# Two softmax attentions with the scores one turn earlier, and transposes and copies signalled one head at a time

## The chip, the core and the metric

The kernel runs on one core of a Trainium2 chip. TensorE (PE), VectorE (DVE), ScalarE (ACT), GpSimd (POOL) and SyncE (SP) each work through a queue of their own, in order, and wait for one another through counting semaphores. The metric is the device time of one execution in microseconds (us). A profiled execution gives, beside that, the start and the duration of every instruction.

## What is computed

Two transformer blocks run one after the other on 512 tokens of width 1024. The first block has, among other things, a chunked attention with a relative bias (8 heads, here called the first attention); the second has a windowed attention with shared keys and a sink (16 heads, the second attention). Both are a softmax over scores plus a table, times values:

```python
# first block, per head; bias is looked up by clipped distance, valid masks chunks ahead
scores = jnp.einsum('bhcqd,bhckd->bhcqk', qc, kb)
scores = jnp.where(valid[None, None, :, None, :], scores + bias[None, :, None], -jnp.inf)
probs = jax.nn.softmax(scores, axis=-1)
out = jnp.einsum('bhcqk,bhckd->bhcqd', probs, vb)
...
# second block, per block of 128 queries
logits = jnp.einsum('bqkgd,bskd->bkgqs', qi, ks).astype(jnp.float32) * scale + bias
logits = jnp.where(valid, logits, NEG_INF)
m = jnp.maximum(logits.max(-1), sink_f)
p = jnp.exp(logits - m[..., None])
denom = p.sum(-1) + jnp.exp(sink_f - m)
o = jnp.einsum('bkgqs,bskd->bqkgd', p, vs.astype(jnp.float32))
o = o / denom.transpose(0, 3, 1, 2)[..., None]
```

Around them stand dense layers (projections, a gated feed-forward layer, a convolution branch) and a product-key expert layer, which together take most of the time and which the change does not touch.

## The kernel before

Weights come from memory as a stream of 128x1024 slots through a ring of four buffers; ACT and POOL split each slot into a high and a low part, and PE multiplies three times for each product. All stages run one after the other in one program. During the two attentions the stream stands still, since its ring is full and nothing consumes it: POOL has nothing to do there, and the engines at work are PE, DVE and ACT.

An attention is a list of *pairs*. A pair is two heads (called halves 0 and 1) and one block of 128 queries. Four pairs (query blocks 0 to 3) make a *group*. In the first attention there are 16 pairs, and the number of keys n of a group's pairs is 128, 256, 384 and 512. In the second there are 32 pairs with n of 256, 384, 384 and 256. All three engines run a loop over *turns*, and each turn works on several pairs at once, in an order written out by hand in three functions of the name `attention(st)`:

- **DVE**, turn p: for both halves *logit* (L862: adds the table to the scores in PSUM, writes `pr`, keeps the maximum), then the small steps on the maxima (L867, or L870 and L871 with a sink), which raise `maxed`; then for pair p-1 the reciprocal of the sum (L878) and *norm* (L881, two instructions, each raises `normed`). A logit waits for `score`, and, since `pr` has three buffers (`PAIRS_PR`), for `turned` of pair p-3.
- **ACT**, turn p: *exp* (L500, two instructions, plus L502 for a sink) of pair p once `maxed` is there; then *copy* (L512) of the transposed probabilities of pair p-2 from banks 6 and 7 (one bank for each half) to `pT`, after `turned` of that pair and `mixed` of pair p-4. The second copy raises `turned_sb`. After a group's last pair, ACT copies the finished heads out (L518). It also issues the DMA of the next group's table.
- **PE**, turn p: *scores* (L1353) of pair p into banks 4 and 5 or 0 and 1 by the parity of p, after the logits of pair p-2; *transposes* (L1364) of pair p-2 into banks 6 and 7, after `turned_sb` of pair p-3 (the banks are free) and `normed` of its own half; *mix* (L1375, probabilities times values) of pair p-3 after `turned_sb` of that pair.

Since each queue is in order, a wait of one instruction holds everything behind it. On PE that means: scores of pair p+1 come behind the transposes of pair p-2 and the mix of pair p-3.

Of the kernel before, what the change touches and what calls it, by code (L numbers as in the profile page):

```python
# [26 lines left out]
ACT = mybir.ActivationFunctionType  # L27
AX_X = mybir.AxisListType.X

P = 128  # L30
# [93 lines left out]
PAIRS_PR = 3  # L124
# [37 lines left out]
def program(nc, x, stream, gains, consts, rel, gqa, keys, ohc, out):  # L162
    ctx = ExitStack()
    with ctx:
# [282 lines left out]
        def _(act):  # L447
# [39 lines left out]
            def attention(st):  # L487
                s, pairs, sm = st["s"], st["pairs"], st["sm"]
                n = len(pairs)
                for p in range(n + 4):  # L490
# [13 lines left out]
                    v = p - 2  # L504
                    if 0 <= v < n:
                        w = pairs[v]
                        act.wait_ge(s["turned"], v + 1)
                        if v >= 2:

                            act.wait_ge(s["mixed"], v - 1)  # L510
                        for half in (0, 1):
                            e = act.activation(st["pT"][:, v % 2, half, :w["n"]], B[6 + half][:, :w["n"]], ACT.Copy)  # L512
                        e.then_inc(s["turned_sb"], 1)
                    v = p - 4
                    if v >= 0 and v % TT == TT - 1:
                        w = pairs[v]
# [273 lines left out]
        def _(dve):  # L790
# [54 lines left out]
            def attention(st):  # L845
                s, pairs, sm = st["s"], st["pairs"], st["sm"]
                n = len(pairs)
                for p in range(n + 1):
                    if p < n:
# [7 lines left out]
                        dve.wait_ge(s["score"], p + 1)  # L857
                        if p >= PAIRS_PR:

                            dve.wait_ge(s["turned"], p - PAIRS_PR + 1)  # L860
                        for half in (0, 1):
                            dve.tensor_tensor_reduce(out=st["pr"][:, p % PAIRS_PR, half, :w["n"]], in0=B[SCORES[p % 2][half]][:, :w["n"]],  # L862
                                                     in1=st["tbl"][g % 2][:, half, w["c0"]:w["c0"] + w["n"]], scale=1.0, scalar=-3.0e38,
# [380 lines left out]
        def _(pe):  # L1244
# [98 lines left out]
            def attention(st):  # L1343
                s, pairs = st["s"], st["pairs"]
                n = len(pairs)
                for p in range(n + 3):
                    if p < n:
                        w = pairs[p]
                        if p >= 2:

                            pe.wait_ge(s["logit"], 2 * p - 2)
                        for half in (0, 1):
                            m = pe.matmul(B[SCORES[p % 2][half]][:, :w["n"]], st["qk"][ROWS[half], w["q"], w["i"] * P:(w["i"] + 1) * P],  # L1353
                                          st["qk"][ROWS[half], w["k"], w["k0"]:w["k0"] + w["n"]], start=True, stop=True)
                        m.then_inc(s["score"], 1)
                    v = p - 2
                    if 0 <= v < n:
                        w = pairs[v]
                        if v >= 1:
                            pe.wait_ge(s["turned_sb"], v)  # L1360
                        for half in (0, 1):
                            pe.wait_ge(s["normed"], 2 * v + half + 1)
                            for c in range(0, w["n"], P):
                                m = pe.transpose(B[6 + half][:, c:c + P], st["pr"][:, v % PAIRS_PR, half, c:c + P], ident)  # L1364
                        m.then_inc(s["turned"], 1)
                    v = p - 3
                    if v >= 0:
                        w = pairs[v]
                        pe.wait_ge(s["turned_sb"], v + 1)
                        if w["group"] >= 2 and v % TT == 0:  # L1370
                            pe.wait_ge(s["head_out"], w["group"] - 1)
                        nb = w["n"] // P
                        for b in range(nb):
                            for half in (0, 1):
                                m = pe.matmul(B[2 + w["group"] % 2][ROWS[half], w["i"] * P:(w["i"] + 1) * P],  # L1375
                                              st["v"][:, w["k0"] // P + b, w["v"][half]:w["v"][half] + HD],
                                              st["pT"][:, v % 2, half, b * P:(b + 1) * P], start=b == 0, stop=b == nb - 1,
                                              skip_group_check=True)
                        m.then_inc(s["mixed"], 1)
# [375 lines left out]
```

## Time and profile before

| | us |
|---|---|
| time, median of 3 runs (lowest to highest) | 2940.41 (2938.57 to 2943.82) |
| the profiled execution's own time | 2938.94 |
| its span from first to last instruction | 2937.1 |
| PE busy over the span | 2767.3 (94%) |
| DVE busy | 1657.0 (56%) |
| ACT busy | 841.9 (29%) |
| POOL busy | 1157.6 (39%) |
| first attention, from its first logit to its last copy-out | 268.7 to 319.3 |
| second attention, likewise | 1085.5 to 1179.4 |

Busy shares over the whole span say little about the attentions, which are 5% of it. A line of the timeline reads: start and duration in us, engine, source line, operation, output tile <- input tiles, shape, how many instructions were merged, and in brackets the idle time of the engine before it and what ended that. Matmuls overlap in the pipeline, so that the time from the start of one group of matmuls to the start of the next (its pitch) says more than their durations. PEld is PE's weight load, which runs beside the matmuls.

### The profile page before, as it was taken

Reading aid. Unit: us, or ns where it says so; the run is one execution under the profiler, and the core shown is the slowest. Engines: PE = TensorE matmul, PEld = TensorE weight load, DVE = VectorE, ACT = ScalarE, POOL = GpSimd, SP = SyncE. Lnnn points to the kernel's source line nnn. Section 1 sums busy time; section 2 is a strip of 40 time slices with the busy share of each in tenths; the row PEclk is TensorE's granted clock in tenths of the full one; section 3 lists DMA queues with packets and bytes.
Section 4 is the critical chain, followed back from the end, with each engine's and each line's share of the span. In section 5 each row is a group of like instructions: output and inputs, shape, how many; then the busy total and the mean of one; then the engine's idle time right before and its main releaser. Section 6 shows DMA issues by size and latency. Waiting matters only on the chain.

```text
span 2937.1 us, 38574 instructions
## 1 busy us (share of the span) xinstructions
PE 2767.3 (94%) x13164; PEld 2188.6 (75%) x13164; DVE 1657.0 (56%) x3297; ACT 841.9 (29%) x1285; POOL 1157.6 (39%) x976
## 2 busy tenths in 40 slices
PE   6997899999999987999999999999999999999997
PEld 5863478878788764778777777888888888888775
DVE  4135642111599537469999956444444444444787
ACT  1133323322222427123445521222222222222111
POOL 4410155555455430453410044444444444444442
PEclk9988999999999999999999999999999999999998
DMA  4210033323223220222346764443443443443442
GB/s 141 88 36 22 15 94 95 98 93 100 87 93 94 78 88 28 65 89 79 94 151 236 253 196 140 114 129 113 115 129 110 119 128 109 120 124 112 128 129 64
DMA packets 208200, 315.44 MB, mean 107 GB/s; under 512 B 139888, under 2 KB 142320, under 8 KB 203888
## 3 DMA queue, kind: packets, MB, share of 16 engines
q1 hardware_dynamic: 63792, 233.34, 25.5%
q10 hardware_dynamic: 144320, 80.94, 10.0%
q8 instruction: 53, 0.87, 0.1%
q14 instruction: 35, 0.29, 0.0%
HBM read 275.45 MB, written 38.80 MB: 107 GB/s over the span
## 4 chain that ended last, share of the span: by engine, by line
PE 43%; issue 23%; DVE 18%; POOL 14%; ACT 1%; DMA 0%; DVEq 0%; ACTq 0%; POOLq 0%
POOL lo L431 14%; PE bank L1247 14%; PE bank L1248 14%; PE bank L1249 14%; DVE ohg L1173 3%; DVE bank L1200 1%; DVE oh L1169 1%; DVE oh L1170 1%; DVE WH L1202 1%; DVE lo L1181 1%; DVE eq L1146 1%; DVE idx L1088 1%; DVE idx L1080 1%; DVE scb L1081 1%; PE bank L1364 1%
## 5 line engine op out<-in xcount | busy, mean ns | idle before, releaser
L431 POOL TENSOR_TENSOR lo<-raw,hi 128x256 fp32r<-128x256 f32 (+1 forms) x972 | 1157.4, 1218 | 1741.5 <-ACT hi L457 911.9
L1247 PE MATMUL bank<-inH,hi 128*128 128x512 f32 x2240 | 893.9, 399 | 28.4 <-DVE inL L798 15.9
L1248 PE MATMUL bank<-inL,hi 128*128 128x512 f32 x2240 | 879.9, 393 | 0.0
L1249 PE MATMUL bank<-inH,lo 128*128 128x512 f32 x2240 | 879.6, 393 | 0.0
L1208 DVE TENSOR_TENSOR xT<-xT,bank 128x512 f32<-128x512 f32 x504 | 339.6, 685 | 538.4 <-PE bank L1249 538.4
L1247 PEld LDWEIGHTS bank<-inH,hi 128*128 128x128 f32 x2240 | 425.6, 190 | 125.9 <-issue 32.9
L1249 PEld LDWEIGHTS bank<-inH,lo 128*128 128x128 f32 x2240 | 425.0, 190 | 90.7
L1248 PEld LDWEIGHTS bank<-inL,hi 128*128 128x128 f32 x2240 | 426.2, 190 | 88.1 <-issue 2.2
L1247 PE MATMUL bank<-WH,hi 128*128 128x512 f32 x1024 | 408.5, 399 | 14.9 <-DVE xT L1208 14.9
L1248 PE MATMUL bank<-WL,hi 128*128 128x512 f32 x1024 | 404.0, 395 | 0.0
L1249 PE MATMUL bank<-WH,lo 128*128 128x512 f32 x1024 | 400.5, 391 | 0.0
L457 ACT ACTIVATE hi<-raw 128x1024 fp32r<-128x1024 f32 x232 | 243.6, 1056 | 483.4 <-PE bank L1249 441.1
L726 ACT ACTIVATE hi<-raw 128x1024 fp32r<-128x1024 f32 x180 | 184.9, 1054 | 455.3 <-PE bank L1249 455.3
L1247 PEld LDWEIGHTS bank<-WH,hi 128*128 128x128 f32 x1024 | 192.2, 188 | 69.1 <-DVE xT L1208 23.6
L1249 PEld LDWEIGHTS bank<-WH,lo 128*128 128x128 f32 x1024 | 192.0, 188 | 48.3
L1248 PEld LDWEIGHTS bank<-WL,hi 128*128 128x128 f32 x1024 | 192.2, 188 | 42.1
L1200 DVE TENSOR_TENSOR bank<-A,Gd 128x512 f32<-128x512 f32 x128 | 142.5, 1114 | 18.1 <-DMA Gd<-gates 15.0
L1008 DVE SCALAR_TENSOR_TENSOR bank<-u,gn,bank 128x512 f32<-128x512 f32 x224 | 148.2, 748 | 0.0
L737 ACT ACTIVATE A<-bank 128x512 f32 (+1 forms) x84 | 50.3, 599 | 318.5 <-PE bank L1249 196.7
L978 DVE TENSOR_TENSOR rt<-sq,bank 128x512 f32<-128x512 f32 x22 | 15.1, 688 | 177.0 <-PE bank L1249 177.0
L961 DVE TENSOR_TENSOR xT<-xT,bank 128x512 f32<-128x512 f32 x24 | 16.5, 687 | 138.5 <-PE bank L1249 138.3
L1202 DVE TENSOR_SCALAR WH<-bank 128x512 fp32r<-128x512 f32 x128 | 88.5, 692 | 4.4
(205 smaller groups left out, 2430.3 us busy)
## 6 DMA issues: line engine op xcount, KB each, us to landing
raw<-stream SPq DMA_DIRECT2D x440, 512.0 KB, 3.6
Gd<-gates ACTq DMA_DIRECT2D x32, 1024.0 KB, 7.4
gates<-stage_a ACTq DMA_DIRECT2D x16, 1024.0 KB, 4.3
gates<-stage_b ACTq DMA_DIRECT2D x16, 1024.0 KB, 4.2
tbl<-gqa ACTq DMA_DIRECT2D x8, 384.0 KB, 3.3
spilled<-res ACTq DMA_DIRECT2D x12, 256.0 KB, 3.1
A<-spilled ACTq DMA_DIRECT2D x6, 512.0 KB, 3.7
xT<-x SPq DMA_DIRECT2D x1, 2048.0 KB, 8.8
```

What stands on the lines that cost most here:

```text
L431: ins = pool.tensor_tensor(lo[:, r, part], raw[:, r, part], hi[:, r, part].bitcast(F32), ALU.subtract)
L457: act.activation(hi[:, r % RING, :], raw[:, r % RING, :], ACT.Copy).then_inc(hi_done, 1)
L726: act.activation(hi[:, r, :], raw[:, r, :], ACT.Copy).then_inc(hi_done, 1)
L737: act.activation(A[:, bass.ds(slot + e, 1), :].rearrange("p a t -> p (a t)"), B[6 + e][:, :], ACT.Gelu).then_inc(gelu_done, 1)
L1008: done.append(chain.mark(dve.scalar_tensor_tensor(to, *tap(j), d, ALU.mult, ALU.add)))
L1173: ins = dve.tensor_tensor(ohg[:, r, part, :, :, :], oh1[:, :, :, :], by_key(gpart[:, part, tok]), ALU.mult)
L1200: chain(dve.tensor_tensor(w[:, :].rearrange("p (b t) -> p b t", t=SPILL), a, Gd[:, buf, :, 2 * wpar + e, :], ALU.mult))
L1202: chain(dve.tensor_scalar(h, w[:, :], 1.0, None, ALU.mult))
L1208: dve.tensor_tensor(xT[:, k, :], xT[:, k, :], B[k % 4][:, :], ALU.add).then_inc(y_added, 1)
L1247: pe.matmul(bank, wh, xh, start=start, stop=False)
L1248: pe.matmul(bank, wh, xl, start=False, stop=False)
L1249: return pe.matmul(bank, wl, xh, start=False, stop=stop_)
```

## The change

PE's loop starts one turn earlier (at -1) and issues the scores of pair p+1 in turn p, ahead of the transposes of pair p-2, still after the logits of the pair that used the same banks (p-1). The scores are then three turns ahead of the transposes instead of two.

Transposes raise `turned` once for each half instead of once for a pair, and ACT's copy of a half waits for its own half alone, and raises `turned_sb` for it. PE's transposes of a half wait for the copy of that half of the pair before. Waits for a whole pair count twice as far. DVE's program keeps its order; one of its waits has another number. No arithmetic changes, and no instruction that computes is added or taken away.

```diff
@@ ACT, attention @@
                         w = pairs[v]
-                        act.wait_ge(s["turned"], v + 1)
                         if v >= 2:
 
                             act.wait_ge(s["mixed"], v - 1)
                         for half in (0, 1):
-                            e = act.activation(st["pT"][:, v % 2, half, :w["n"]], B[6 + half][:, :w["n"]], ACT.Copy)
-                        e.then_inc(s["turned_sb"], 1)
+                            act.wait_ge(s["turned"], 2 * v + half + 1)
+                            act.activation(st["pT"][:, v % 2, half, :w["n"]], B[6 + half][:, :w["n"]], ACT.Copy).then_inc(s["turned_sb"], 1)
@@ DVE, attention @@
                         if p >= PAIRS_PR:
 
-                            dve.wait_ge(s["turned"], p - PAIRS_PR + 1)
+                            dve.wait_ge(s["turned"], 2 * (p - PAIRS_PR + 1))
@@ PE, attention @@
-                for p in range(n + 3):
-                    if p < n:
-                        w = pairs[p]
-                        if p >= 2:
-
-                            pe.wait_ge(s["logit"], 2 * p - 2)
+                for p in range(-1, n + 3):
+                    if p + 1 < n:
+                        w, b = pairs[p + 1], (p + 1) % 2
+                        if p >= 1:
+
+                            pe.wait_ge(s["logit"], 2 * p)
                         for half in (0, 1):
-                            m = pe.matmul(B[SCORES[p % 2][half]][:, :w["n"]], st["qk"][ROWS[half], w["q"], w["i"] * P:(w["i"] + 1) * P],
+                            m = pe.matmul(B[SCORES[b][half]][:, :w["n"]], st["qk"][ROWS[half], w["q"], w["i"] * P:(w["i"] + 1) * P],
                                           st["qk"][ROWS[half], w["k"], w["k0"]:w["k0"] + w["n"]], start=True, stop=True)
                         m.then_inc(s["score"], 1)
                     v = p - 2
                     if 0 <= v < n:
                         w = pairs[v]
-                        if v >= 1:
-                            pe.wait_ge(s["turned_sb"], v)
                         for half in (0, 1):
+                            if v >= 1:
+                                pe.wait_ge(s["turned_sb"], 2 * v + half - 1)
                             pe.wait_ge(s["normed"], 2 * v + half + 1)
                             for c in range(0, w["n"], P):
                                 m = pe.transpose(B[6 + half][:, c:c + P], st["pr"][:, v % PAIRS_PR, half, c:c + P], ident)
-                        m.then_inc(s["turned"], 1)
+                            m.then_inc(s["turned"], 1)
                     v = p - 3
                     if v >= 0:
                         w = pairs[v]
-                        pe.wait_ge(s["turned_sb"], v + 1)
+                        pe.wait_ge(s["turned_sb"], 2 * v + 2)
```

What stands in PE's queue in the second attention, in the turn that transposes a pair of 256 keys (n of 256, its two halves in banks 6 and 7). Before, with the mix and the next scores behind it:

```order
L1353 MATMUL bank4<-qk2_77 128x384 [waits logit2]
L1353 MATMUL bank5<-qk2_77 128x384
L1364 MATMUL bank6<-cs_56,pr2_81 128x128 [waits normed2,turned_sb2]
L1364 MATMUL bank6<-cs_56,pr2_81 128x128
L1364 MATMUL bank7<-cs_56,pr2_81 128x128 [waits normed2]
L1364 MATMUL bank7<-cs_56,pr2_81 128x128
L1375 MATMUL bank2<-pT2_82,v2_78 64x128 [waits turned_sb2]
L1375 MATMUL bank2<-pT2_82,v2_78 64x128 x3
L1353 MATMUL bank0<-qk2_77 128x256 [waits logit2]
L1353 MATMUL bank1<-qk2_77 128x256
```

Now (the same lines of code stand one number lower):

```order
L1352 MATMUL bank0<-qk2_77 128x256 [waits logit2]
L1352 MATMUL bank1<-qk2_77 128x256
L1363 MATMUL bank6<-cs_56,pr2_81 128x128 [waits normed2,turned_sb2]
L1363 MATMUL bank6<-cs_56,pr2_81 128x128
L1363 MATMUL bank7<-cs_56,pr2_81 128x128 [waits normed2,turned_sb2]
L1363 MATMUL bank7<-cs_56,pr2_81 128x128
L1374 MATMUL bank2<-pT2_82,v2_78 64x128 [waits turned_sb2]
L1374 MATMUL bank2<-pT2_82,v2_78 64x128 x3
L1352 MATMUL bank4<-qk2_77 128x256 [waits logit2]
L1352 MATMUL bank5<-qk2_77 128x256
```

The scores into banks 0 and 1, which stood behind these transposes and this mix, now stand ahead of them, and the second half's transposes have a second wait.

ACT's queue in the second attention, from a pair's last exp (L502) over the two copies to the next pair's exp. Before:

```order
L502 ACTIVATE sm2_85<-sm2_85 128x2
L512 ACTIVATE pT2_82<-bank6 128x256 [waits mixed2,turned2]
L512 ACTIVATE pT2_82<-bank7 128x256
L500 ACTIVATE pr2_81,sm2_85<-pr2_81,sm2_85 128x384 [waits maxed2]
L500 ACTIVATE pr2_81,sm2_85<-pr2_81,sm2_85 128x384
```

Now:

```order
L502 ACTIVATE sm2_85<-sm2_85 128x2
L512 ACTIVATE pT2_82<-bank6 128x256 [waits turned2,mixed2]
L512 ACTIVATE pT2_82<-bank7 128x256 [waits turned2]
L500 ACTIVATE pr2_81,sm2_85<-pr2_81,sm2_85 128x384 [waits maxed2]
L500 ACTIVATE pr2_81,sm2_85<-pr2_81,sm2_85 128x384
```

The order is the same; the second copy has a wait of its own.

## Rows read from the trace of the kernel before

**Rows 1.** Sums of each attention: stretch, length, each engine's busy us, clock, DMA.

```profile
268.70:319.30 50.60, 38.58 (x300) 23.38 (x296) 29.60 (x131) 31.70 (x100) 0.00 (x0) 0.91 0.07 22
1085.50:1179.40 93.90, 71.73 (x604) 44.23 (x600) 68.45 (x321) 66.37 (x233) 0.00 (x0) 0.96 0.09 27
```

**Rows 2.** Waits in the second attention: who waited for whom, total, times, longest.

```profile
PEld bank L1364 <- ACT pT L512: 34.3, 30, 2.6
...
DVE pr L862 <- PE bank L1353: 14.9, 21, 2.7
```

**Rows 3.** The chain of waits, second attention, in order of time: start, us, what.

```profile
1120.57 0.87 PE bank L1353 x4
...
1121.46 0.56 DVE pr L862
...
1124.33 0.55 ACT pT L512 x2
...
1124.92 0.66 PE bank L1364 x4
```

**Rows 4.** Timeline of DVE, second attention: first logit instruction of seven of its pairs.

```profile
1085.50 0.42 DVE L862 CUSTOM_DVE_ANT_0 pr<-bank,tbl 128x256 f32<-128x256 f32 x1 [0.86 <-PE bank L1353]
...
1086.58 0.55 DVE L862 CUSTOM_DVE_ANT_0 pr<-bank,tbl 128x384 f32<-128x384 f32 x1
...
1088.85 0.55 DVE L862 CUSTOM_DVE_ANT_0 pr<-bank,tbl 128x384 f32<-128x384 f32 x1
...
1091.25 0.42 DVE L862 CUSTOM_DVE_ANT_0 pr<-bank,tbl 128x256 f32<-128x256 f32 x1
...
1152.43 0.42 DVE L862 CUSTOM_DVE_ANT_0 pr<-bank,tbl 128x256 f32<-128x256 f32 x1 [1.06 <-PE bank L1353]
...
1163.67 0.42 DVE L862 CUSTOM_DVE_ANT_0 pr<-bank,tbl 128x256 f32<-128x256 f32 x1 [1.07 <-PE bank L1353]
...
1171.63 0.42 DVE L862 CUSTOM_DVE_ANT_0 pr<-bank,tbl 128x256 f32<-128x256 f32 x1
```

**Rows 5.** Timeline of PE, first attention, two stretches in which it hardly waited.

```profile
276.53 0.88 PE L1364 MATMUL bank<-cs,pr 128*128 128x128 f32 x6 [1.11 <-ACT pT L512]
277.33 0.66 PE L1375 MATMUL bank<-pT,v 128*64 128x128 f32 x8
277.92 0.70 PE L1353 MATMUL bank<-qk 64*128 64x256 f32 x4
278.55 1.09 PE L1364 MATMUL bank<-cs,pr 128*128 128x128 f32 x8
...
306.37 0.92 PE L1353 MATMUL bank<-qk 64*128 64x384 f32 x4
307.22 0.44 PE L1364 MATMUL bank<-cs,pr 128*128 128x128 f32 x2
```

**Rows 6.** Timeline of PE: first and last line of two stretches at the slower pace.

```profile
288.02 1.31 PE L1364 MATMUL bank<-cs,pr 128*128 128x128 f32 x6 [2.27 <-ACT pT L512]
...
292.59 0.88 PE L1375 MATMUL bank<-pT,v 128*64 128x128 f32 x12
...
1092.30 1.54 PE L1364 MATMUL bank<-cs,pr 128*128 128x128 f32 x6 [2.24 <-ACT pT L512]
...
1097.39 0.88 PE L1375 MATMUL bank<-pT,v 128*64 128x128 f32 x12
```

**Rows 7.** Timeline of DVE, first attention: first logit of pairs 0, 4 and 15.

```profile
268.73 0.29 DVE L862 CUSTOM_DVE_ANT_0 pr<-bank,tbl1a 128x128 f32<-128x128 f32 x1 [0.70 <-PE bank L1353]
...
275.56 0.29 DVE L862 CUSTOM_DVE_ANT_0 pr<-bank,tbl1b 128x128 f32<-128x128 f32 x1 [0.19 <-DVE tbl1b L856]
...
309.79 0.69 DVE L862 CUSTOM_DVE_ANT_0 pr<-bank,tbl1b 128x512 f32<-128x512 f32 x1 [0.48 <-PE bank L1353]
```

**Rows 8.** Timeline of ACT: the last pair's copies, first and second attention.

```profile
316.41 1.08 ACT L512 ACTIVATE pT<-bank 128x512 f32<-128x512 f32 x2 [1.18 <-PE bank L1364]
...
1177.35 0.66 ACT L512 ACTIVATE pT<-bank 128x256 f32<-128x256 f32 x2 [0.75 <-PE bank L1364]
```

## The prediction

> **What bounds the kernel now.** I read the sums of the two attentions first, then the waits in them, then the chain of waits, then the timelines of DVE and PE. The attentions take 50.6 and 93.9 us, and no engine is full there: in the second PE is busy for 71.7, DVE for 68.5 and ACT for 66.4 us of 93.9 [rows 1]. So a loop of waits sets the pace. The waits say which: PE's transposes stand for 34.3 us until ACT's copies free banks 6 and 7, and DVE's logits stand for 14.9 us until scores are there [rows 2]. The chain of waits closes the loop: scores start at 1120.57, the logits at 1121.46, the copies behind that pair's exps are under way at 1124.33, and the transposes start at 1124.92 [rows 3]. Behind the transposes stand a mix and the next scores, and only those let DVE go on. One such round is 1124.92 - 1120.57 = 4.35 us, plus transposes and mix of four and eight pieces, 2 x 0.59 (below) and a little issue time: about 5.6 us, and it moves the loop by two turns. That fits the 11.24 us which DVE needs for a group of four turns, from 1152.43 to 1163.67 [rows 4], or 2.81 a turn.
>
> **The change part by part.**
>
> *Scores one turn earlier.* The scores of pair p+1 no longer stand behind the transposes of p-2 and the mix of p-3. The path from DVE's logits over exp, copy, transposes, mix and scores back to DVE is as long as before but now moves the loop by three turns: 5.6 / 3 = 1.9 us a turn. It stops being the bound. What is late next is one of three queues, or the wait for a free `pr` buffer.
>
> DVE's queue, where it did not wait for scores: 2.27 us from 1086.58 to 1088.85 (logit 384, norm 256) and 2.40 to 1091.25 (384, 384) [rows 4]. A logit instruction of 256 is 0.13 shorter than one of 384 (0.42 against 0.55 [rows 4]), and there are two, so 256 with 384 is 2.40 - 0.26 = 2.14 and 256 with 256 is 2.27 - 0.26 = 2.01. A group: 8.82 us.
>
> PE's queue, by pitches where it did not wait: six transposes 0.80, a mix of eight 0.59, scores of 256 0.63, scores of 384 0.85 (306.37 to 307.22) [rows 5]. A mix of twelve and six transposes are both busy for 0.88 [rows 5, 6], a mix of eight and four transposes both for 0.66 [rows 3, 5], so I give them the same pitches. A pair of 256 costs 0.63 + 0.59 + 0.59 = 1.81, one of 384 0.85 + 0.80 + 0.80 = 2.45, a group 8.52 us. The first attention has the same mean n (320), so 8.52 there too. ACT: 66.4 / 8 = 8.3 and 31.7 / 4 = 7.9 us a group [rows 1], with small overlaps counted twice.
>
> The three queues are within 6% of each other, so that none will run quite without waits: the widths change from turn to turn, and an engine that is early in a narrow turn is late in a wide one. For that I add 0.2 us a group in the second attention, where DVE leads, and 0.6 in the first, where PE leads: 9.0 and 9.1 us a group.
>
> *The wait placed ahead.* Scores of p+1 wait for the logits of p-1, and the transposes of p-2, the mix of p-3 and through them ACT's copies are now queued behind that wait. It should be free: those transposes need norm of p-2, which on DVE comes after the logits of p-1. The scores' own 0.63 to 0.85 us delay the transposes by less than DVE takes between these logits and the end of that norm (max steps, reciprocal and norm, the rest of a turn of 2.4 us beyond about 1.1 us of logits).
>
> *Signals by half.* The added waits and increments are one each on PE and ACT a turn. In the trace PE already has a wait between the halves (for `normed`), and six transposes with it take 0.80 us, no more than a mix of twelve without, so a wait that is already met costs near nothing; the upper bound is the gap of 0.15 to 0.2 us that PE shows between a group of matmuls with a wait ahead and the one before (six transposes at 0.11 and a gap are 0.80). I take nothing, and keep 0.15 a turn for the range. For the increments the Trainium skill has a rule that speaks against this part (TensorE: Matmul & The Clock Gate, The cost: per-tile semaphore tail): increments serialize, at about 26 ns each. By it the 48 more would be worth 1.3 us at most; no row here shows an increment by itself. What the halves gain: the copy of half 0 starts while half 1 is still transposed, and the next transposes start after the first copy. In the loop this is slack. In the tail it is on the path: the last copies wait 1.18 and 0.75 us for transposes [rows 8], and the two last pairs run transposes and copies strictly in turn. I take 0.9 us from the first tail and 0.7 from the second.
>
> *The slow stretches.* At 288.02 PE needs 4.57 us until 292.59 for what otherwise takes 0.80 + 0.59 + 0.63 + about 1.0 = 3.0, and at 1092.30 5.09 until 1097.39 for 0.80 + 0.59 + 0.63 + 0.80 = 2.8 [rows 5, 6]. Both fit the lower of the two clocks (1.2 against 2.4 GHz), as do mean granted clocks of 0.91 and 0.96 [rows 1]. They cost 1.5 and 2.3 us of PE work; I take two stretches in the first attention (the mean clock has room for them), 3.0, and 2.3 in the second. Today part of that is slack; with PE nearly full it is all on the path. I assume that they stay.
>
> *Sum.* Second attention, first to last logit: now 1171.63 - 1085.50 = 86.1 us, of which 5.8 until 1091.25 is a start that doesn't wait [rows 4]. After: 5.8 + 7 x 9.0 + 2.3 = 71.1, so 15.0 less; with the tail 15.7 less. First attention: now 309.79 - 268.73 = 41.1, of which 6.8 until 275.56 [rows 7]. After: 6.8 + 2 x 9.1 + three turns of the last group (3/4 x 9.1 = 6.8) + 3.0 = 34.8, so 6.3 less; with the tail 7.2. Together 22.9 us. Nothing else fills that time: POOL and the weight stream stand still in both, so nothing they do later depends on how long the attentions take. The profiled execution goes from 2938.9 to 2916.0; the median of the runs is 1.5 above that execution, which gives 2917.5 us.
>
> **The rivals.**
>
> *PE becomes the bound.* If each added wait costs 0.15 us, PE's group is 8.52 + 4 x 0.15 = 9.1, and with 0.5 of unevenness 9.6 instead of 9.0 and 9.1: 7 x 0.6 + 2.75 x 0.5 = 5.6 us more, 2923. For it: PE is only 0.3 below DVE in a group. Against it: the pitch of six transposes with a wait between halves.
>
> *The buffer of `pr` becomes the bound.* Logit p waits for the transposes of p-3, that is logit p, exp p, copies of p-2, transposes of p-1, logit p+2. From 1121.46 to 1124.92 is 3.46 us, plus transposes of 0.66 [rows 3]: 4.1 for two turns, 8.2 a group, below DVE's 8.8. With widest pairs in a row it comes to some 4.5, against 4.67 of DVE for its two widest turns. If it binds at each group's wide turns, with 0.8 a group: 0.6 x 9.75 = 6 us more, again 2923; the two are told apart by who waits.
>
> *The lead does nothing.* Where PE's scores of p+1 still come late, since the mix of p-4 ahead of them waits for copies that come after the exp of p-2, only the halves help: some 0.3 us of copy and transposes in each round of two turns, 24 rounds, and the tails: 2940.4 - 7.2 - 1.6 = 2932. Against it: that mix belongs to a turn which is over when DVE reaches logit p-1, by the chain.
>
> *The clock (slower).* With PE at its lower clock a turn costs 2 x 8.52 / 4 = 4.26 us instead of 2.25, since PE is then the bound by far. Eleven or twelve turns more than now at that clock (23 / 2.0) eat the whole gain, and all 48 would end at some 3010. At 20 turns more the time is 2917.5 + 40 = 2958. What speaks for it is that slow stretches do come in the attentions, after PE has waited over 2 us [rows 6]; against it, that the change takes such waits away, and that between the stretches transposes run at their faster pitch. The Trainium skill (TensorE: Matmul & The Clock Gate, Part 4: PE-mode transpose) says that transposes don't count as work that holds the clock up. By that the denser loop would not hold the clock better, as about a third of its PE time is transposes; the trace has both attentions mostly at the higher clock with that same third.
>
> **How the numbers follow.** Forecast 0.70: 2917.5. PE bound or `pr` bound, 0.2 together: 2923. The lead does nothing, 0.04. Slower by the clock, 0.03. The rest, 0.03, is a gain beyond the range. The range: without any unevenness (0.2 x 7 + 0.6 x 2.75 = 3.1 us) and without slow stretches (5.3) the time is 2909; with the second or third case and one more slow stretch of 2.3 us elsewhere it is 2926. All but 0.1 lies between 2909 and 2926. A measurement of this kernel can tell about 0.2% (5.9 us) from no change, so faster means below 2934.5: 0.95. Same 0.02, slower 0.03.
>
> **What would show it.** In the new profile the logits' wait for scores (14.9 us in the second attention) should be nearly gone, and the transposes' wait for copies should fall from 34.3 to below 12. DVE's group in the second attention should be 8.8 to 9.2 us, with its longest idle in front of a logit below 0.4. PE's busy time in the attentions should stay the same in us. The second attention should last some 78 us, the first 43. I am wrong if PE shows idle in front of scores (its wait for logits), if ACT's copies wait for PE in mid-loop, if more of the attentions runs at the slower pitch, or if the groups fall to 9 us and the whole does not, which would mean that the slower clock came elsewhere.

## The result and the profile after

| | before | changed |
|---|---|---|
| median of the runs, us | 2939.5 (2938.6 to 2943.8, 4 runs) | 2907.9 (2906.1 to 2909.6, 4 runs) |
| the profiled execution's span | 2937.1 | 2907.7 |
| first attention, first logit to last copy-out | 50.6 | 39.9 |
| second attention, likewise | 93.9 | 74.4 |

The changed kernel takes 0.9884 of the time before, 95% interval 0.9869 to 0.9899: 31.6 us less where 22.9 were forecast. The direction and the mechanism were right; the time lies 1.1 us below the forecast range.

In the two profiles the attentions are 10.7 and 19.5 us shorter, 30.2 together, and the spans differ by 29.4. The other 0.8 us is a sum of both signs outside the attentions: 2.0 less ahead of the first logit, 1.1 more between the attentions, 1.6 more behind the second. That is code which the change does not touch. Yet the 1.1 us come again from profile to profile: over all thirteen profiles of this document, the part between the attentions takes 766.2 to 766.3 us in the three whose first attention runs as before, and 767.1 to 767.9 in the eight others with three `pr` buffers. In the 30.7 us behind the first attention the mean granted clock is 0.89 before and 0.83 in the changed kernel, so it is likely that a little of what the clock gives inside the attention is taken back behind it. The 1.6 us tell nothing: a second profile of the changed kernel has 3.5 us less there than the first.

The sums of the attentions (stretch, length, busy us of PE, PEld, DVE, ACT and POOL, granted clock, DMA share, GB/s), to be held against [rows 1]:

```profile
266.70:306.63 39.93, 35.11 (x300) 21.65 (x298) 29.63 (x131) 31.20 (x100) 0.00 (x0) 0.96 0.09 27
1073.96:1148.35 74.39, 68.08 (x604) 42.73 (x600) 66.16 (x320) 65.47 (x233) 0.00 (x0) 1.00 0.11 34
```

The instructions are the same and DVE and ACT are as long busy as before; what has gone is waiting. PE is busy for 3.5 us less in the first attention and 3.7 in the second, although it does the same work: the mean granted clock rose from 0.91 to 0.96 in the first attention and from 0.96 to 1.00 in the second, so that in the latter nothing is left of the stretch at the lower of the two levels (1.2 GHz). What keeps the first at 0.96 is a stretch that began ahead of it: the clock is 0.51 from 266.7 to 269.7 us and 1.00 from there to the attention's end.

The waits in the second attention, as in [rows 2]:

```profile
PEld bank L1363 <- ACT pT L512: 17.4, 31, 1.8
...
PE bank L1363 <- ACT pT L512: 4.0, 9, 1.4
...
DVE pr L861 <- PE bank L1352: 0.9, 1, 0.9
```

DVE's wait for scores fell from 14.9 us to one wait of 0.9, at the very start. PE's weight loads still wait 17.4 us for copies, and PE's matmuls 4.0: PE is now early and stands because DVE sets the pace. DVE's timeline shows that it does, first logits of two groups in a row, as [rows 4]:

```profile
1099.45 0.42 DVE L861 CUSTOM_DVE_ANT_0 pr<-bank,tbl 128x256 f32<-128x256 f32 x1
...
1101.45 0.55 DVE L861 CUSTOM_DVE_ANT_0 pr<-bank,tbl 128x384 f32<-128x384 f32 x1
...
1103.72 0.55 DVE L861 CUSTOM_DVE_ANT_0 pr<-bank,tbl 128x384 f32<-128x384 f32 x1
...
1106.12 0.42 DVE L861 CUSTOM_DVE_ANT_0 pr<-bank,tbl 128x256 f32<-128x256 f32 x1
...
1108.25 0.42 DVE L861 CUSTOM_DVE_ANT_0 pr<-bank,tbl 128x256 f32<-128x256 f32 x1
```

The turns are 2.00, 2.27, 2.40 and 2.13 us, a group 8.80, against 11.24 before, and no line has an idle time in brackets. All whole groups but the first (7.89) are like this to 0.01 us. The chain of waits agrees: between 1100 and 1110 us it lies on DVE from line to line, with ACT and PE nowhere in it (start, us, what):

```profile
1099.88 0.34 DVE pr L861
...
1100.92 0.36 DVE pr L880 x2
1101.28 0.17 issue
1101.45 0.55 DVE pr L861
```

In the first attention a group is 9.10 us, and there DVE still waits, in each group at the same places:

```profile
277.78 0.56 DVE L861 CUSTOM_DVE_ANT_0 pr<-bank,tbl1b 128x384 f32<-128x384 f32 x1 [0.89 <-PE bank L1363]
...
280.02 0.69 DVE L861 CUSTOM_DVE_ANT_0 pr<-bank,tbl1b 128x512 f32<-128x512 f32 x1 [0.27 <-PE bank L1363]
```

The releaser is L1363, the transposes, not the scores (L1352): the logit waits for its `pr` buffer.

The last thing to see is PE at the start of the second attention, where the kernel before had its slow stretch [rows 6]:

```profile
1077.20 0.70 PE L1363 MATMUL bank<-cs,pr 128*128 128x128 f32 x4 [0.35 <-DVE pr L880]
...
1080.50 0.87 PE L1363 MATMUL bank<-cs,pr 128*128 128x128 f32 x6 [1.39 <-ACT pT L512]
1081.31 0.66 PE L1374 MATMUL bank<-pT,v 128*64 128x128 f32 x8
1081.89 0.92 PE L1352 MATMUL bank<-qk 64*128 64x384 f32 x4
1082.74 0.88 PE L1363 MATMUL bank<-cs,pr 128*128 128x128 f32 x6
1083.55 0.88 PE L1374 MATMUL bank<-pT,v 128*64 128x128 f32 x12
```

The waits of 1.48 and 2.24 us ahead of the first two groups of transposes have become 0.35 and 1.39, and the transposes behind them run at the faster pace: six in 0.81 us, where before they took 1.47 there (1092.30 to 1093.77). There is no slow stretch left in either attention's loop.

### The profile page after: what moved, and what is told of

Same layout as the page of the kernel before. It is cut to its first block, busy times and chain, and to the rows that moved or that the text cites. A ratio compares the mean times of both kernels' runs of the same rounds, so it can differ in the third digit from the quotient of the medians.

```text
span 2907.7 us, 38620 instructions
## 1 busy us (share of the span) xinstructions
PE 2761.2 (95%) x13164; PEld 2186.6 (75%) x13164; DVE 1655.4 (57%) x3297; ACT 840.4 (29%) x1285; POOL 1157.1 (40%) x976
## 4 chain that ended last, share of the span: by engine, by line
PE 43%; issue 23%; DVE 18%; POOL 14%; DMA 0%; DVEq 0%; ACT 0%; ACTq 0%; POOLq 0%
PE bank L1246 14%; POOL lo L431 14%; PE bank L1247 14%; PE bank L1248 14%; DVE ohg L1172 2%; DVE bank L1199 1%; DVE oh L1168 1%; DVE oh L1169 1%; DVE WH L1201 1%; DVE pr L861 1%; DVE lo L1180 1%; DVE eq L1145 1%; DVE idx L1087 1%; DVE idx L1079 1%; DVE scb L1080 1%
## 5 line engine op out<-in xcount | busy, mean ns | idle before, releaser
L1246 PE MATMUL bank<-WH,hi 128*128 128x512 f32 x1024 | 408.8, 399 | 14.9 <-DVE xT L1207 14.9
```

The source lines that it names most:

```text
L1246: pe.matmul(bank, wh, xh, start=start, stop=False)
```

## The experiments

Theory A: the earlier scores carry the gain, DVE's queue is the next bound, and the slow stretches of PE are set off by its own waits, so that they go with them. Rivals: the halves carry it; PE or ACT bound; the slow stretches were missing by chance. In each experiment "group" is the time from a group's first logit to the next group's, read from DVE's timeline. The runs were made in four comparisons, each with the kernel before beside it, whose median was 2939.5, 2939.6, 2943.7 and 2939.8 us; so medians of different comparisons (a to d in the table) are held against each other by the ratio to before and its 95% interval.

| | median us (runs) | ratio to before (interval) | first attention | second attention | group, first | group, second |
|---|---|---|---|---|---|---|
| before | 2939.5 (4), a | | 50.6 | 93.9 | 11.3, 12.9 | 11.25 |
| changed | 2907.9 (4), a | 0.9884 (0.9869 to 0.9899) | 39.9 | 74.4 | 9.10 | 8.80 |
| changed, again | 2906.2 (5), d | 0.9888 (0.9873 to 0.9903) | 39.9 | 74.4 | 9.10 | 8.80 |
| lead alone | 2913.7 (4), b | 0.9914 (0.9898 to 0.9931) | 42.6 | 77.9 | 9.37 | 8.99 |
| halves alone | 2930.2 (10), b | 0.997 (0.996 to 0.9979) | 47.0 | 89.7 | 11.1, 12.2 | 10.76 |
| second attention alone | 2918.9 (4), b | 0.9935 (0.9919 to 0.9952) | 50.6 | 74.4 | 11.3, 12.9 | 8.80 |
| changed, four `pr` buffers | 2912.1 (4), b | 0.9906 (0.989 to 0.9923) | 38.4 | 74.4 | 8.63 | 8.80 |
| before, PE's waits filled, second | 2938.3 (10), c | 0.9987 (0.9978 to 0.9997) | 50.5 | 92.2 | 11.3, 12.9 | 11.25 |
| before, PE's waits filled, first | 2935.0 (1), d | | 49.0 | 93.9 | 11.3, 11.5 | 11.25 |
| changed, PE stalled in 3 turns | 2911.9 (2), c | 0.9895 (0.9874 to 0.9917) | 39.9 | 82.0 | 9.10 | 8.80 |
| changed, one DVE step more | 2916.6 (1), c | | 39.9 | 81.9 | 9.10 | 9.61 |
| changed, half of norm on GpSimd | 2905.3 (4), c | 0.9872 (0.9855 to 0.989) | 39.9 | 73.0 | 9.10 | 8.69 |
| the same and four buffers | 2906.0 (4), d | 0.9882 (0.9866 to 0.9898) | 38.4 | 71.4 | 8.63 | 8.53 |

### The lead alone

The kernel before with the scores a turn earlier; the signals stay whole:

```diff
-                for p in range(n + 3):
-                    if p < n:
-                        w = pairs[p]
-                        if p >= 2:
-                            pe.wait_ge(s["logit"], 2 * p - 2)
+                for p in range(-1, n + 3):
+                    if p + 1 < n:
+                        w, b = pairs[p + 1], (p + 1) % 2
+                        if p >= 1:
+                            pe.wait_ge(s["logit"], 2 * p)
...
```

> The scores one turn earlier, but turned and turned_sb raised once for a pair as before. Theory A (the lead carries the gain; the halves matter only where transposes and copies run strictly in turn): second attention bound by DVE's own queue, 8.8 to 8.9 us a group, its tail 0.6 longer than with the whole change; first attention 9.3 to 9.5 us a group, since there logit 384 waits for the transposes of the pair of 512, which now wait for both copies. In all 2 to 3 us above the whole change, about 2910.5. Rival B (the halves are needed in the loop, PE's transposes stay behind both copies): groups of 9.3 and more in the second attention, 2915 or more. On the slow stretches of PE: if long waits of PE set them off, none inside either attention; if they were absent by chance, they may be back.

It takes 0.9914 of the time before (0.9898 to 0.9931). The groups came out as theory A says or a tenth above, 8.99 and 9.37. The 8.99 comes from one turn of four, 2.18 us instead of 2.00, in which the logit also waits for transposes, that is for its `pr` buffer. The total is 3 us above that forecast, and the attentions say why. No slow stretch was expected inside either attention, and two were back, one behind a longer wait of PE at the start of the second attention, one in the first one's tail. PE's timeline in the second attention:

```profile
1084.66 0.87 PE L1364 MATMUL bank<-cs,pr 128*128 128x128 f32 x6 [1.66 <-ACT pT L512]
1085.47 0.66 PE L1375 MATMUL bank<-pT,v 128*64 128x128 f32 x8
1086.06 1.49 PE L1353 MATMUL bank<-qk 64*128 64x384 f32 x4
1087.48 1.54 PE L1364 MATMUL bank<-cs,pr 128*128 128x128 f32 x6
```

The wait is 1.66 us where the whole change has 1.39. The six transposes at 1087.48 run at the slower pace, and that group took 10.53 us instead of 8.99.

### The halves alone

The changed kernel with the scores where the kernel before has them:

```diff
-                for p in range(-1, n + 3):
...
+                for p in range(n + 3):
+                    if p < n:
+                        w = pairs[p]
+                        if p >= 2:
+                            pe.wait_ge(s["logit"], 2 * p - 2)
...
```

> Signals by half, but the scores where they were. Theory A: the loop of waits over scores, logits, exp, copy, transposes and mix stays and is shortened by the overlap of one half, 0.2 to 0.3 us a round of two turns: groups of 10.6 to 10.8 us in the second attention, PE still waits 1.5 us and more at its start; in all 5 to 7 us below the kernel before, about 2933. If long waits of PE set off its slow stretches, one stays in the second attention about 8 us after its start and one or two in the first. If the halves carried more than the lead: 2925 or less.

0.997 of the time before (0.996 to 0.9979), 9.4 us less by the medians where 5 to 7 were expected. DVE's logits of the second attention, first pair of two groups in a row:

```profile
1102.23 0.42 DVE L861 CUSTOM_DVE_ANT_0 pr<-bank,tbl 128x256 f32<-128x256 f32 x1 [0.40 <-issue]
...
1112.98 0.42 DVE L861 CUSTOM_DVE_ANT_0 pr<-bank,tbl 128x256 f32<-128x256 f32 x1 [0.55 <-issue]
```

10.75 us a group, as expected, with DVE idle in front of its logits: the loop over scores is still there. A slow stretch stayed in each attention. By the medians the lead alone brings 25.9 us, the halves alone 9.4, both 31.6: the halves are worth less once the lead is there. In the profiles the lead alone is 6.3 us of attention behind the whole change: 2.1 in the two loops, where DVE waits for transposes, 1.8 in the tails, and 2.4 by the two slow stretches.

### The second attention alone

The changed kernel, whose first attention has PE's loop and the signals of the kernel before. In ScalarE's turn, and in PE's program:

```diff
+                        new = st is stage2
...
+            def attention(st):
+                (attention_new if st is stage2 else attention_old)(st)
```

> The whole change in the second attention, the old order and signals in the first. The profiles give 19.5 us less for the second attention and 10.7 for the first, so 2920 to 2921 if both parts are real and add up. If slow stretches come from PE's waits, the first attention keeps one or two (about 22 and 35 us after its first score), the second has none. If the first attention's slow stretches were gone by chance in the changed kernel, they can be gone here too, and the first attention lasts 47 us instead of 50.6.

The two parts add up: 20.7 us by the medians, 19.5 by the attention. And the first attention repeats that of the kernel before to 0.01 us, slow stretches included: groups of 11.34, 12.92 and 9.97 (three turns). So these stretches are no accident of one execution, and their going in the changed kernel isn't either: all six profiles whose second attention has both parts of the change, and neither a stall nor a further DVE step, have a mean granted clock of 1.00 there.

### Filling PE's waits in the kernel before

Two kernels put useless matmuls in the places where PE waits, which changes nothing else. In the second attention:

```diff
                         m.then_inc(s["score"], 1)
+                    if st is stage2 and p in (2, 3):
+                        for _ in range(4 if p == 2 else 8):
+                            pe.matmul(B[3][:, :P], ident, ident, start=True, stop=True)
```

> The kernel before, with twelve more matmuls of 128x128 (identity by identity, into bank 3, whose contents aren't used) in PE's queue behind the scores of pairs 2 and 3 of the second attention, where PE otherwise waits 1.5 and 2.2 us; the result doesn't use them. Theory A (PE's waits at the start of the attention set off its slow stretch): no slow stretch at 7 to 11 us after the first logit; the second attention's first group takes 8 to 9 us instead of 10.7 and the attention is some 2 us shorter, though PE does more. Rival B (the slow stretch comes from elsewhere or by chance): it is still there, the attention lasts 93.9 us or a little more. The total moves by 2 us at most, less than its spread.

PE's timeline, the same place as the stretch from 1092.30 in [rows 6] (L1358 is the filling):

```profile
1090.66 2.05 PE L1358 MATMUL bank<-cs 128*128 128x128 f32 x16
1092.97 0.87 PE L1367 MATMUL bank<-cs,pr 128*128 128x128 f32 x6 [0.26 <-ACT pT L512]
1093.78 0.66 PE L1378 MATMUL bank<-pT,v 128*64 128x128 f32 x8
```

Six transposes in 0.81 us instead of 1.47: the slow stretch has gone, and the first group took 9.04 us instead of 10.69, though PE did more. All other groups stayed at 11.25. The first attention kept its two stretches. A new slow stretch came 1.5 us behind the second attention. By the medians the total is 5.4 us below before (ratio 0.9987), where at most 2 were expected and the attention gives 1.65; the rest stays unexplained.

In the first attention:

```diff
                         m.then_inc(s["score"], 1)
+                    if st is stage1 and p in (8, 12):
+                        for _ in range(8):
+                            pe.matmul(B[2 + (p - 3) // TT % 2][:, 3 * P:], ident, ident, start=True, stop=True, skip_group_check=True)
```

> The kernel before, with eight more matmuls (128x128, identity by identity, into columns of the mix's bank that are written later) behind the scores of pairs 8 and 12 of the first attention, where PE otherwise waits 2.3 and 2.2 us ahead of its two slow stretches. Theory A: both slow stretches are gone, groups of 12.92 and 9.97 us become about 11.4 and 8.4, and the attention is 3 us shorter. Rival B: they stay where they are.

```profile
293.28 2.05 PE L1358 MATMUL bank<-cs 128*128 128x128 f32 x16
295.61 0.87 PE L1367 MATMUL bank<-cs,pr 128*128 128x128 f32 x6 [0.29 <-ACT pT L512]
296.42 0.66 PE L1378 MATMUL bank<-pT,v 128*64 128x128 f32 x8
297.00 0.70 PE L1353 MATMUL bank<-qk 64*128 64x256 f32 x4
...
307.11 0.87 PE L1367 MATMUL bank<-cs,pr 128*128 128x128 f32 x6 [2.69 <-ACT pT L512]
```

Both stretches of the loop have gone (the groups 11.50 and 8.96), and one came in the tail, behind a wait of 2.69 us that nothing filled. So the attention became only 1.6 us shorter, half of what was expected.

### Stalling PE in the changed kernel

```diff
                         pe.wait_ge(s["turned_sb"], 2 * v + 2)
+                        if st is stage2 and p in (3, 4, 5):
+                            pe.wait_ge(s["logit"], 2 * (p + 2))
```

> The changed kernel with a wait of PE more in turns 3, 4 and 5 of the second attention: before each of these mixes PE waits for the logits of the next pair but one, which costs it 1 to 1.5 us a turn. Theory A: PE's waits early in the attention bring the slow stretch back, some 4 to 8 us after the first logit, and it costs about 2.3 us beside the waits themselves; first groups of 11 us or more instead of 7.9 and 8.8. Rival B: no slow stretch, groups longer by the waits alone, 1 to 3 us in all.

```profile
1080.28 0.88 PE L1363 MATMUL bank<-cs,pr 128*128 128x128 f32 x6 [1.39 <-ACT pT L512]
1082.55 1.12 PE L1376 MATMUL bank<-pT,v 128*64 128x128 f32 x8 [1.39 <-DVE sm L861]
1083.60 1.65 PE L1352 MATMUL bank<-qk 64*128 64x384 f32 x4
1085.18 1.54 PE L1363 MATMUL bank<-cs,pr 128*128 128x128 f32 x6
```

The slow stretch is back and lasted from 1082.55, 9 us behind the first logit, to about 1092: the second group took 16.33 us instead of 8.80. Of these 7.5 us the three waits are 4.1 (1.39, 1.34 and 1.34); the rest goes with the slower pace, by which PE is busy for 3.9 us longer in this attention (71.9 for 68.1). With the filling this shows both directions: take PE's waits away and the stretch goes, put waits in and it comes.

### One step more on DVE

```diff
                         chain(dve.reciprocal(sm[:, b, 4, :], sm[:, b, 2, :]))
+                        if st is stage2:
+                            chain(dve.tensor_scalar(sm[:, b, 6, :], sm[:, b, 4, :], 1.0, None, ALU.mult))
```

> The changed kernel with one more step of 128x2 elements on DVE in each turn of the second attention (a copy of the reciprocals that nothing reads), about 0.20 us with its wait. If DVE's queue is the bound there, the group grows from 8.80 to about 9.6 us and the attention from 74.4 to 80.5. If DVE had slack that the profile hides, or PE or ACT are the real bound, less than a third of that.

Two logits four turns apart, both of a group's last pair:

```profile
1110.29 0.42 DVE L861 CUSTOM_DVE_ANT_0 pr<-bank,tbl 128x256 f32<-128x256 f32 x1
...
1119.91 0.42 DVE L861 CUSTOM_DVE_ANT_0 pr<-bank,tbl 128x256 f32<-128x256 f32 x1
```

9.62 us against 8.80, four times 0.20: DVE had no slack. The attention is 1.4 us longer than expected, as its second group took 11.07 us, in another slow stretch of PE, from 1078.5 to 1085:

```profile
1078.49 1.23 PE L1354 MATMUL bank<-qk 64*128 64x256 f32 x4 [0.51 <-DVE sm L861]
```

No such stretch was expected. The scores at 1078.49 already run at the slower pace, and no wait of PE in the attention before them is above 0.78 us; against the changed kernel one wait is longer, 0.55 us instead of 0.35. So the changed kernel goes free of the stretch by a small margin.

### Four buffers of `pr`

```diff
-PAIRS_PR = 3
+PAIRS_PR = 4
```

> The changed kernel with four buffers of pr instead of three. In its profile DVE's logits wait 4.0 us in nine places of the first attention for transposes. If the third buffer bounds the first attention (9.1 us a group), it falls towards PE's own queue of 8.5 a group: 2 us less, about 2906. If PE's queue is the bound already, no change. The second attention, where DVE's queue is full, stays at 8.8 a group.

The third buffer was the bound of the first attention: with a fourth the group is 8.63, PE's queue, and what DVE waits for is scores again:

```profile
281.61 0.69 DVE L861 CUSTOM_DVE_ANT_0 pr<-bank,tbl1b 128x512 f32<-128x512 f32 x1 [0.93 <-PE bank L1352]
```

The first attention became 1.4 us shorter, and the kernel did not: its median is 4 us above that of the changed kernel, in another comparison and with overlapping intervals (0.989 to 0.9923 and 0.9869 to 0.9899). In its profile the stages between the attentions took 771.1 us instead of 767.3. That question comes back with the last pair.

### Half of norm on GpSimd, and with four buffers

In the second attention DVE multiplies half 0 alone, and GpSimd half 1, released by the reciprocal; PE's transposes of half 1 wait for GpSimd. GpSimd's loop over the weight slots is split in two for it, before and behind the multiplications, and DVE's last reciprocal waits for one of them:

```diff
-                        for half in (0, 1):
+                        for half in (0,) if st is stage2 else (0, 1):
...
+                            if st is stage2:
+                                pe.wait_ge(normed_b if half else s["normed"], v + 1)
...
+            for v, w in enumerate(pairs2):
+                pr = pr2[:, v % PAIRS_PR, 1, :w["n"]]
+                pool.wait_ge(inverse, v + 1)
+                pool.tensor_scalar(pr, pr, sm2[:, v % 2, 4, 1:2], None, ALU.mult).then_inc(normed_b, 1)
```

> The changed kernel with norm of half 1 on GpSimd instead of DVE in the second attention, GpSimd being idle there. DVE's queue loses 0.27 to 0.34 us a turn, 1.2 a group, so PE's queue (8.52) and ACT's (8.2) bound: groups of 8.5 to 8.6 and the attention 1.5 to 2 us shorter. Rival: GpSimd is slow at this (1 us or more for 384) or holds DVE up while it reads and writes SBUF, the transposes of half 1 come late, and groups are 9 us or more.

```profile
L451 POOL TENSOR_SCALAR pr<-pr,sm x32: 998/1275/1472, 1077.1 to 1143.2; 128x256 f32<-128x256 f32 x16, 128x384 f32<-128x384 f32 x16
```

GpSimd takes 1.08 us for 256 and 1.47 for 384, four times what DVE takes (0.27 and 0.34 by pitch), but that fits in a turn. Groups fell only to 8.69, because now transposes of half 1 come later and DVE waits for its `pr` buffer (4.6 us in 14 places). The second attention is 1.3 us shorter where 1.5 to 2 were expected, and the ratio to before, 0.9872, can't be told from that of the changed kernel. So the buffers were the next thing to add (`PAIRS_PR = 4`, and from the third pair on DVE's reciprocal waits for GpSimd's multiplication two pairs back):

> Norm of half 1 on GpSimd in the second attention, as before, and four buffers of pr. The waits left in front of DVE's logits were, in both attentions, waits for transposes, so a fourth buffer should take them: second attention from 8.69 to about 8.55 us a group (PE's queue 8.52), first from 9.10 to 8.63. Total 2.5 us below the run with GpSimd alone and 4 to 5 below the changed kernel. If the buffers don't matter once GpSimd is in the loop, 8.69 stays and only the first attention gains 1.4 us.

The attentions did as expected: 8.53 and 8.63 us a group, PE's queue, with the second attention 3.0 us and the first 1.4 us shorter than in the changed kernel. PE ran through without waiting, here a group of four turns, 8.53 us from 1099.65 to 1108.18:

```profile
1099.65 0.70 PE L1374 MATMUL bank<-qk 64*128 64x256 f32 x4
...
1101.67 0.92 PE L1374 MATMUL bank<-qk 64*128 64x384 f32 x4
...
1104.13 0.92 PE L1374 MATMUL bank<-qk 64*128 64x384 f32 x4
...
1106.37 0.70 PE L1374 MATMUL bank<-qk 64*128 64x256 f32 x4
...
1108.18 0.70 PE L1374 MATMUL bank<-qk 64*128 64x256 f32 x4
```

But the median, 2906.0, is that of the changed kernel in the same comparison, 2906.2. In the profiles the 4.4 us were given back between the attentions, which took 772.0 us instead of 767.3, at a mean granted clock of 0.97 instead of 0.98. PE's timeline shows one of the places, the last part of the first block's feed-forward layer. First the kernel with GpSimd and four buffers, then the changed kernel in its second profile:

```profile
628.56 0.79 PE L1268 MATMUL bank<-actH,hi 128*128 128x512 f32 x1 [2.77 <-DVE actL L1003]
629.15 0.63 PE L1269 MATMUL bank<-actL,hi 128*128 128x512 f32 x1
629.57 0.63 PE L1270 MATMUL bank<-actH,lo 128*128 128x512 f32 x1
```

```profile
629.75 0.50 PE L1246 MATMUL bank<-actH,hi 128*128 128x512 f32 x1 [2.77 <-DVE actL L981]
630.09 0.41 PE L1247 MATMUL bank<-actL,hi 128*128 128x512 f32 x1
630.33 0.39 PE L1248 MATMUL bank<-actH,lo 128*128 128x512 f32 x1
```

The same wait of 2.77 us, the same instructions behind it; in the first kernel matmuls follow one another by 0.43 us for the next 5.7 us, in the second by 0.24. So not each such wait brings a slow stretch. That the stage now starts at another time could decide it; no run here sets that time alone, so it stays open. The two kernels with four buffers both lost some 4 us between the attentions, and none of the other eleven profiles did (766.2 to 767.9 us).

### The changed kernel again

> The changed kernel again, beside the others. Its attentions should be as in the first profile to 0.1 us: groups of 8.80 and 9.10, no slow stretch in either loop. Outside of them, slow stretches of PE are expected to differ by up to 3 us from profile to profile, as the stage ahead of the first attention did (11.5 us of slow pace in some profiles, 17.5 in others, with the same code). If that part is not chance but belongs to the change, it is again the shorter one here.

0.9888 of the time before (0.9873 to 0.9903), and both attentions to 0.03 us as in the first profile. Ahead of the first attention, PE's code is the same in all kernels, and yet the profiles are of two kinds. The sums from 60 us to the first logit, before and changed:

```profile
60.00:268.73 208.73, 191.83 (x836) 129.34 (x836) 59.67 (x113) 54.79 (x101) 54.99 (x79) 0.90 0.18 56
```

```profile
60.00:266.78 206.78, 189.88 (x841) 129.33 (x841) 59.71 (x114) 54.78 (x101) 56.01 (x80) 0.92 0.18 56
```

The difference is the clock, 0.90 against 0.92, and PE is busy for 2 us longer for the same work. Of thirteen profiles three have the longer stretch there: before, "four `pr` buffers" and "filled, second", that is kernels with and without the change. So the 2.0 us of it in the 29.4 between the first two profiles do not belong to the change.

## Why the prediction was right and wrong

**The bound of before and the mechanism: right.** The loop over scores, logits, exp, copy, transposes and mix was the bound; with the lead it is gone, and the halves alone leave it.

**DVE's queue as the next bound: right to 0.02 us.** 8.82 us a group was worked out from four unhindered turns, 8.80 measured, and a step of 0.20 us more on DVE costs 0.20 a turn.

**The allowance for unevenness: wrong in the second attention.** 0.2 us a group were added, 1.4 in all; the loop has none. With queues of 8.8, 8.5 and 8.2 us it ran at the longest one's pace, and so it did at PE's once half of norm and the `pr` buffer were out of the way (8.53 for the 8.52 worked out).

**The first attention's group: right number by luck, wrong reason.** 9.1 was PE's 8.5 plus 0.6 of unevenness. PE's queue is 8.63 there (the group with four buffers), and what makes 9.10 of it is the wait for the `pr` buffer, the second rival, which was put at 0.8 us a group and takes 0.47.

**Waits and increments by half cost nothing: right.** Six transposes with two waits between the halves and an increment more take 0.81 us (1082.74 to 1083.55), as they do with whole signals (1092.97 to 1093.78 in the filled kernel). The 26 ns for each increment of the Trainium skill (TensorE: Matmul & The Clock Gate, The cost: per-tile semaphore tail) don't show in that pitch.

**The slow stretches: this is the step that failed.** "I assume that they stay" put 3.0 and 2.3 us into the sum. The same text had seen that they came after PE had waited over 2 us, and that the change takes such waits away; it used this against the slower rival only and not for the forecast. They went: the loops have none in any profile of the changed kernel, and the filled and the stalled kernels show that they hang on PE's waits. How near the border is, the lead alone and the further DVE step show, which each have a stretch again behind waits longer by 0.2 to 0.3 us. The Trainium skill (TensorE: Matmul & The Clock Gate, Part 4: PE-mode transpose) says that a transpose doesn't count as PE being busy in the same way and doesn't bring the full clock. The trace doesn't bear out the use that the prediction made of it: a third of PE's time in the second attention is transposes, and its mean granted clock is 1.00. No run here has transposes alone.

**Tails: near.** 1.1 and 0.7 us shorter, 0.9 and 0.7 forecast. The last copies' waits fell from 1.18 and 0.75 us [rows 8] to 0.63 and 0.62:

```profile
303.75 1.09 ACT L512 ACTIVATE pT<-bank 128x512 f32<-128x512 f32 x2 [0.63 <-PE bank L1363]
...
1146.33 0.66 ACT L512 ACTIVATE pT<-bank 128x256 f32<-128x256 f32 x2 [0.62 <-PE bank L1363]
```

**What was said would show it.** DVE's wait for scores did go (14.9 to 0.9 us), DVE's group is 8.80 without idle time, and ACT's copies wait for PE in the tails alone. Three signs missed: the transposes' wait for copies fell from 34.3 to 17.4 us and not below 12; PE's busy time fell by 3.5 and 3.7 us instead of staying, which is the slow stretches; and the attentions last 74.4 and 39.9 us, not 78 and 43, which is in the main the same.

**The sum.** The attentions became 7.3 us shorter than forecast: 5.3 by the slow stretches, 1.4 by unevenness, 0.4 by the first attention's start and last group, 0.2 by the tails. From the forecast 2917.5 that leads to 2910.2. Of the rest to 2907.9, 0.9 us is a median of before that came out lower with a fourth run; 1.4 us stays open, as it is in the medians alone, and the two profiles differ by 0.8 us the other way outside the attentions.

**The range.** Its lower end, 2909, was worked out as "without any unevenness and without slow stretches", and most of that happened: no slow stretches in the loops, no unevenness in the second attention, but in the first a wait of the same size as its allowance. The range ended just there, with nothing added for stages outside the attentions that vary by 2 us and more, and with the chance of that case put far too low.

## What to carry to other kernels

Where three engines work in turns on a list, sum each queue's unhindered pitches over one period: here the loop ran at the largest sum once no wait on another engine was left in front of that queue (8.80 us for 8.82, 8.53 for 8.52), and nothing had to be added for unevenness. Before costing what stays, ask whether the waits that go were also what lets TensorE's clock fall: that gain or loss comes on top, here 5.3 us that the forecast held back. And when a gain in a small stage does not show in the total, look for slow stretches elsewhere in the profile before doubting the stage.

## What the runs showed of the hardware

- A slow stretch of PE (matmuls at half pace, for 3 to 10 us) could be taken out of a loop by useless matmuls in the waits ahead of it: 1.65 us gained in the second attention and 2.4 in the first one's loop. Each time another stretch came soon after, in the first attention's tail and 1.5 us behind the second attention.
- Waits of 1.39 us brought none in the changed kernel, and in "lead alone" one came behind a wait of 1.66 us; with one DVE step more, one came with no wait above 0.78 us in the attention before it; a wait of 2.77 us brought one in one kernel and none in another. The length of the wait alone does not decide it.
- GpSimd multiplies 128x384 f32 by a scalar for each partition in 1.47 us and 128x256 in 1.08, beside a DVE whose own steps did not become longer (a logit instruction of 384 at 0.56 and 0.55 us as before).
